# A fused decoder step on one core: first projections from the raw input, norm factor applied to their results, convolution stores moved to GpSimd

## The reference, cut to what matters

```python
xn = rmsnorm(x, g_attn_norm)                     # x * r * g,  r = rsqrt(mean(x*x) + eps), per row
z = jnp.einsum('bsd,de->bse', xn, w_in)          # qa, ka, va, oa, ia, fa, cq, ckv, kr, gate_a, gate_b
q_b = jnp.einsum('bsc,che->bshe', rmsnorm(cq, g_q_a), w_uq)
c_kv = rmsnorm(ckv, g_kv_a); k_rope = rope(kr, pos)
...                                              # mLSTM branch, latent attention branch, gates, W_out
u = jnp.einsum('bsd,df->bsf', rmsnorm(h, g_ffn_norm), w_up)
ext = jnp.concatenate([prev, u], axis=1)         # causal convolution of width 3
out = jnp.einsum('bsf,fd->bsd', silu(gate) * val, w_down)
return x + f, ..., ext[:, -2:]                   # the last two rows are the new convolution state
```

## Time and profile before

| | |
|---|---|
| median of 3 runs | 2778.37 us (2778.24 to 2780.13) |
| profiled execution | 2775.73 us, span 2773.9 us |
| PE busy | 98% (19156 instructions) |
| DVE, ACT, POOL busy | 59%, 46%, 15% |
| mean granted clock of PE | 0.995 |
| first 16 products of the warm-up | 2.88 to 11.68 us |
| DMA | 393.53 MB, mean 142 GB/s |

### The profile page before, as it was taken

How to read it: one execution, slowest core, us unless ns; L and a number is a source line. 1 busy time by engine, 2 the same in 40 slices (tenths; PEclk the granted TensorE clock), 3 DMA queues, 4 the chain that set the end, 5 groups by cost and what they waited for, 6 DMA issues and landing times.

```text
span 2773.9 us, 54080 instructions
## 1 busy us (share of the span) xinstructions
PE 2731.4 (98%) x19156; PEld 2603.6 (94%) x19156; DVE 1640.6 (59%) x2739; ACT 1281.2 (46%) x2286; POOL 404.3 (15%) x762
## 2 busy tenths in 40 slices
PE   9998899999999999999999999999999999999999
PEld 9865799999999979999999999999999999999999
DVE  5466776666666654555454344466677645677744
ACT  5536665565556544444453333344444433444422
POOL 0102343343334310000000000022000000000000
PEclk9999899999999999999999999999999999999999
DMA  7524112212122177656567576576555556555475
GB/s 240 199 70 107 38 46 55 67 49 61 50 63 63 38 236 208 198 171 188 179 177 208 162 172 169 166 192 176 165 165 158 146 164 188 167 162 165 140 175 133
DMA packets 743252, 393.53 MB, mean 142 GB/s; under 512 B 115374, under 2 KB 725400, under 8 KB 742456
## 3 DMA queue, kind: packets, MB, share of 16 engines
q1 hardware_dynamic: 709132, 378.61, 47.6%
q10 hardware_dynamic: 33916, 12.35, 1.7%
HBM read 370.49 MB, written 22.75 MB: 142 GB/s over the span
## 4 chain that ended last, share of the span: by engine, by line
PE 59%; DVE 1%; ACT 1%; issue 1%; ACTq 1%; DMA 0%; SPq 0%; DVEq 0%
PE bank L302 19%; PE bank L307 19%; PE bank L303 19%; DMA stage<-in_w_in_dram 0%; PE bank L2748 0%; ACT sqm L2812 0%; PE bank L2726 0%; PE bank L2736 0%; ACTq L3382 0%; DVE hn L2913 0%; ACT w_hi_b L283 0%; PE bank L2733 0%; ACTq L3383 0%; PE bank L2722 0%; ACTq L3388 0%
## 5 line engine op out<-in xcount | busy, mean ns | idle before, releaser
L290 DVE TENSOR_TENSOR w_lo_b<-stage,w_hi_b 128x2048 fp32r<-128x2048 f32 (+2 forms) x286 | 612.4, 2142 | 411.2 <-ACT w_hi_b L283 407.2
L283 ACT ACTIVATE w_hi_b<-stage 128x2048 fp32r<-128x2048 f32 (+1 forms) x284 | 508.1, 1790 | 568.0 <-PE bank L307 509.0
L302 PE MATMUL bank<-xnH,w_hi_b 128*128 128x288 f32 (+1 forms) x2736 | 741.1, 299 | 2.7 <-PEq L191 2.5
L303 PE MATMUL bank<-xnL,w_hi_b 128*128 128x288 f32 (+1 forms) x2736 | 735.7, 295 | 0.0
L302 PEld LDWEIGHTS bank<-xnH,w_hi_b 128*128 128x128 f32 (+1 forms) x2736 | 514.0, 188 | 12.4 <-issue 11.4
L303 PEld LDWEIGHTS bank<-xnL,w_hi_b 128*128 128x128 f32 (+1 forms) x2736 | 513.4, 188 | 0.3
L1741 PE MATMUL bank<-uk_all,lat 128*128 128x384 f32 (+1 forms) x1344 | 441.4, 328 | 13.2 <-DVE lat L2535 5.3
L1743 PE MATMUL bank<-uk_all,lat 128*128 128x384 f32 (+1 forms) x1344 | 435.1, 324 | 0.0
L307 PE MATMUL bank<-xnH,w_lo_b 128*128 128x288 f32 (+1 forms) x2736 | 390.8, 295 | 0.0
L307 PEld LDWEIGHTS bank<-xnH,w_lo_b 128*128 128x128 f32 (+1 forms) x2736 | 372.1, 188 | 0.0
L302 PE MATMUL bank<-haH,w_hi_b 128*128 128x288 f32 x1024 | 275.3, 296 | 4.7 <-ACT w_hi_b L283 4.7
(11 more groups left out here) (535 smaller groups left out, 3707.7 us busy)
## 6 DMA issues: line engine op xcount, KB each, us to landing
stage<-in_w_in_dram SPq DMA_DIRECT2D x88, 1024.0 KB, 5.3
stage<-in_w_up_dram SPq DMA_DIRECT2D x88, 1024.0 KB, 5.3
stage<-in_w_down_dram SPq DMA_DIRECT2D x64, 704.0 KB, 4.7
raw<-in_cache_kv_latent_dram SPq DMA_DIRECT2D x256, 64.0 KB, 1.8
stage<-in_w_branch_a_dram SPq DMA_DIRECT2D x16, 1024.0 KB, 5.5
stage<-in_w_branch_b_dram SPq DMA_DIRECT2D x16, 1024.0 KB, 5.4
stage<-in_w_out_dram SPq DMA_DIRECT2D x16, 1024.0 KB, 5.7
vals<-in_cache_kv_latent_dram SPq DMA_DIRECT2D x60, 256.0 KB, 2.9
```

Of the source, the lines that this page charges most:

```text
L283: act.activation(h, a, ACT.Copy).then_inc(w_hi, 1)
L290: dve.tensor_tensor(lo, a, h.bitcast(F32), ALU.subtract).then_inc(w_lo, 1)
L302: pe.matmul(out, hi, xH(k), start=first and k == 0, stop=False)
L303: pe.matmul(out, hi, xL(k), start=False, stop=False)
```

## The change

- The warm-up is 6 products, and the two behind the gain rows go. `turn_x` transposes plain x (one instruction for each of three tiles, `is_transpose`), with no factor r. SP's order is: identity, first feature half of x, sample rows, first half of block 0's weights, second feature half of x, second half of block 0's weights, then the two gain rows, then blocks 1 to 3.
- Blocks 0 to 8 are formed from g * x without r. In the loop over chunks block 1 lags by 12; block 2's high products stand behind block 0's low ones.
- The squares, the root, the reciprocal and the diagonals come later (`norms` on ACT behind block 2's split). A product of ones with the diagonals spreads r over all partitions in bank 4, and DVE copies it to `rx`.
- DVE multiplies each result by `rx` as it reads the bank (`scaled_out`), and ACT squares the scaled one in SBUF (`square`).
- The normed x is made afterwards in four groups of four chunks: GpSimd adds high and low part and multiplies by `rx`, ACT rounds to the new high part, DVE subtracts, and SP stores the halves in eight pieces between the query chunks. ACT's first query evacuation waits for these stores, since the high parts lie in x_reg.
- The transposes of the convolution state lie two each behind the first two blocks of the first pair; its eight stores are issued by GpSimd as soon as they are done.

```diff
@@ SP
+                    x_half(0)
                     sp.dma_start(x_tok[0:N_S, 2, :], A["x_sample"]...).then_inc(x_in2, 16)
+                    first_weights(0, w_first)
+                    x_half(1)
+                    first_weights(1, w_landed[0])
                     sp.wait_ge(rows_zero, 1)
...
-                    chunk(0)
-                    chunk(1)
-                    for i in range(2, 6):
+                    def normed(g):
+                        part = slice(g * XG, (g + 1) * XG)
+                        sp.wait_ge(x_nL, g + 1)
+                        sp.dma_start(xnL_dram[:, part, :], xr[:, part, :]).then_inc(xL_out, 16)
+                        sp.wait_ge(x_nH, g + 1)
+                        sp.dma_start(xnH_dram[:, part, :], xrH[:, part, :].bitcast(F32)).then_inc(xH_out, 16)
+                    for i in range(4):
                         chunk(i)
-                    sp.wait_ge(x_L, KC)
-                    sp.dma_start(xnL_dram, xnL[:].bitcast(F32)).then_inc(xL_out, 16)
-                    chunk(6)
-                    sp.wait_ge(x_H, KC)
-                    sp.dma_start(xnH_dram, xnH[:].bitcast(F32)).then_inc(xH_out, 16)
+                        normed(i)
@@ PE
-                    warm(16)
+                    warm(6)
                     pe.wait_ge(rows_in, 16 * 9)
                     pe.transpose(bank[3][:, 0:60], rows[:], ident[0:60, 0:60]).then_inc(vec_t, 1)
-                    warm(2)
...
-                            tr = pe.matmul(bank[4 + c % 4][:, t0:t0 + n], x_tok[:, t, chunk_], norm_t[:, t, 0:n], start=True, stop=True)
+                            if c % (KC // 2) == 0:
+                                pe.wait_ge(x_in[t][c // (KC // 2)] if t < 2 else x_in2, 16)
+                            tr = pe.transpose(bank[4 + c % 4][:, t0:t0 + n], x_tok[0:n, t, chunk_], ident[0:n, 0:n])
...
+                    for k in range(KC):
+                        pe.wait_ge(x_L, k + 1)
+                        if k + 4 < KC:
+                            turn_x(k + 4)
+                        high_half(0, k)
+                        if k >= LAG:
+                            high_half(1, k - LAG)
+                    for k in range(KC - LAG, KC):
+                        mm = high_half(1, k)
+                    mm.then_inc(x_hb, 1)
+                    low_half(0)
+                    for k in range(KC):
+                        high_half(2, k)
+                    low_half(1)
+                    low_half(2)
+                    pe.wait_ge(x_dg, 3)
+                    pe.matmul(bank[4][:, 0:T], ones, rw[:, 0:T], start=True, stop=True).then_inc(x_rb, 1)
...
-                            pe.wait_ge(z_free[c], i + 1)
+                            pe.wait_ge(c_sq, LC * i + c + 1)
@@ ACT
                     for c in range(KC):
                         high(c)
+                        if c in (1, 4, 8, 11):
+                            quarter_high(0, (1, 4, 8, 11).index(c))
+                    for g in range(4):
+                        quarter_high(2, g)
+                    norms()
...
+                    def square(m):
+                        act.wait_ge(z_free[m % 4], m // 4 + 1)
+                        if m >= 4:
+                            act.wait_ge(a_sum, 1)
+                        act.activation(sqc[:, m % 4, :], (cqT if m < 4 else ckvT)[:, m % 4, :], ACT.Square).then_inc(c_sq, 1)
+                    def normed_high(g):
+                        act.wait_ge(x_nr, g + 1)
+                        act.activation(xrH[:, part, :], xr[:, part, :], ACT.Copy).then_inc(x_nH, 1)
                     for n in range(4, 9):
                         split_hi(act, At(n), width=W0 if n == 8 else P)
-                        small(n - 2)
+                        square(n - 2)
+                        if n > 4:
+                            normed_high(n - 5)
...
+                    square(7)
                     uq_high(0)
-                    small(8)
                     uq_high(1)
                     act.wait_ge(x_out, 32)
+                    act.wait_ge(xL_out, 16 * 4)
+                    act.wait_ge(xH_out, 16 * 4)
@@ GpSimd
+                    pool.wait_ge(x_L, KC)
+                    pool.wait_ge(x_ss, 5)
+                    for g in range(4):
+                        part = slice(g * XG, (g + 1) * XG)
+                        pool.tensor_tensor(xr[:, part, :], xnH[:, part, :].bitcast(F32), xnL[:, part, :].bitcast(F32), ALU.add).then_inc(x_sum, 1)
+                        pool.wait_ge(x_rx, 1)
+                        pool.wait_ge(x_sum, g + 1)
+                        pool.tensor_tensor(xr[:, part, :], xr[:, part, :], rx[:].unsqueeze(1).broadcast_to([P, XG, T]), ALU.mult).then_inc(x_nr, 1)
@@ DVE
                     for n in range(3, 9):
                         split_lo(dve, At(n), width=W0 if n == 8 else P)
+                        if n == 3:
+                            dve.wait_ge(x_rb, 1)
+                            dve.tensor_copy(rx[:], bank[4][:, 0:T]).then_inc(x_rx, 1)
+                            dve.wait_ge(x_rx, 1)
+                            scaled_out(0)
+                            scaled_out(1)
+                        else:
+                            scaled_out(n - 2)
+                        if n > 4:
+                            normed_low(n - 5)
                         if n == 6:
                             latent(0, cqT, G_QA)
...
+                    scaled_out(7)
                     uq_low(0)
+                    scaled_out(8)
                     uq_low(1)
@@ last stage: ACT, GpSimd, DVE
-                            if g and c.i is None and c.c == 2:
-                                conv_out(m)
...
+                pool.wait_ge(c_ev, 4)
+                for q in range(4):
+                    pool.dma_start(conv_s[q], rin[32 * q:32 * q + 2 * NB]).then_inc(cvs_out, 16)
+                    pool.dma_start(conv_p[q], rin[32 * q + CR:32 * q + CR + 2]).then_inc(cvs_out, 16)
...
-                            if g and c.i is None and c.c == 0:
+                            if g and c.i is None and c.c == 0 and m < 2:
                                 dve.wait_ge(u_new, 4 * GRP)
-                                part = slice(m * CQ, (m + 1) * CQ)
-                                dve.transpose(rin[:, part]..., cv[:, part]...).then_inc(c_ev, 1)
+                                for i in (2 * m, 2 * m + 1):
+                                    part = slice(i * CQ, (i + 1) * CQ)
+                                    dve.transpose(rin[:, part]..., cv[:, part]...).then_inc(c_ev, 1)
```

133 lines of the change are left out of this document (57 added, 76 removed).

## The result

The changed kernel takes 2789.11 us in the median (2787.21 to 2793.3, 6 runs), the kernel before 2778.3 (2775.76 to 2782.48, 6 runs): a ratio of 1.0039 (95% interval 1.0027 to 1.0051). It is slower by 10.8 us. The forecast of 2779.2 was 10 us too low, and its range ended at 2787.5. The profiled execution took 2788.91 us with a span of 2787.1, that is 13.2 more span than the profile of before.

The account below looks back on a forecast made before the run. PE, busy 98% of the span, was taken to bound the kernel. The terms -3.8 + 2 + 8.4 + 1 - 6.8 = +0.8 us gave 2776.5 profiled, 2779.2 for a median, range 2771.5 to 2787.5.

Parts of the forecast that it names:

- What bounds the kernel: Whole kernel: PE is busy 98% of the span, so the end moves only by what makes PE do less or wait.
- Work taken off PE: Ahead of block 3: plain transposes at 0.11 us each, 0.33 a turn, make twelve turns cost 4.0 us, not 7.9.
- Start: First turns wait for gain rows landing at 13.3 us; first product at 15.4, block 3 at 39.0, 3.8 earlier.
- rival C: SP's gain rows don't wait behind the weights, turns start near 8 us: -6.2 us, 2772.2; chance 0.05.
- The clock at the start: PE idles from 6.2 to 13.3 us after the shorter warm-up, lowering the clock: +2 us, bounds 0 and 3.3.
- Norm factor and halves: Block 3 to queries: GpSimd and DVE take turns, PE waits 8.4 us more (5.5 to 9.8), plus 1 of clock.
- the 1 before block 8: A PE wait of 1 us before block 8, part of the 8.4 us of new waits.
- Rival B: GpSimd and DVE don't hold each other up in the new order: -8.1 us, 2770.3; chance 0.15.
- Convolution stores: Near the end: eight stores leave ACT's queue, whose issuing delayed PE: gain 6.8 us, bounds 0 and 6.8.
- Rival A: GpSimd's stores take no less from the path, PE waits for weights there: +7.6 us, 2786.0; chance 0.17.
- The sum: All terms together: +0.8 us, 2776.5 for a profiled execution and 2779.2 for a median; forecast's chance 0.55.
- What would show it: Signs in the new trace: block 3's start, stretched low halves, two PE waits, low clock, ACT's issue waits, low-half spacing.

Follow-up runs that it names:

- e5_full_turns: The changed kernel with 24 warm-up products and the third transpose of each turn on 128 rows instead of 32: 2776.13 us, one run.
- e7_rows_first: The changed kernel with SP loading its two gain rows right behind the identity, six warm-up products as in the changed kernel: 2782.97 us, one run.
- e1_warm24: The changed kernel with 24 warm-up products of PE instead of six, nothing else: 2780.52 us, ratio 1.0008 to the kernel before.
- e6_before_short_warm: The kernel before with six warm-up products instead of sixteen, nothing else: 2776.35 us, one run.
- e9_cold_full: The changed kernel with its six warm-up products and the third transpose of each turn on 128 rows: 2777.49 us, one run.

## Why the prediction was wrong, point by point

- **What bounds the kernel.** PE, and the end moves with its start and its waits: right.
- **Work taken off PE** (twelve turns from 7.9 to 4.0). Wrong. 0.11 each is right for transposes with 128-row weights (0.33 a turn in e5_full_turns), but the row it was scaled from the earlier trace rows has no change of row count in it. With the 32-row third one a turn costs 0.59, so twelve are 7.1 and the gain 0.8.
- **Start** (rows at 13.3, first product at 15.4). That the rows come late for their place in SP's order was right (e7_rows_first), and rival C was out. They landed 1.5 later than worked out, and not for the reason given, transfers in order: SP's issue of the first took 4.16, and the second landed 5.1 behind its own issue. With the dearer turns the first product came at 17.9 at full clock (e1_warm24), and block 3 at 43.9 instead of 39.0.
- **The clock at the start** (+2, bounds 0 and 3.3). The step that failed: the clock's loss measured 10.1 us (54.0 less the 43.9 of e1_warm24), three times its upper bound. The bound let about as long a stretch of work run at the low level as PE had been idle, as the earlier trace rows had it, where dense products follow the idle time (its 6.6 us are 7.1 by the prediction's own 6.2 and 13.3). The prediction said itself that no row shows how soon the clock returns, and bounded it all the same; no rival stood for a longer stay. Here the clock stayed low for as long as the loop ran, 25 us. The bound should have been the whole loop at the low level. With 128-row weights the term would have been about right: 3.5 in e6_before_short_warm, 1.7 in e9_cold_full.
- **Norm factor and halves** (8.4, bounds 5.5 to 9.8, and +1 of clock): right in mechanism and place; the size is partly luck. GpSimd's instructions took 2.68 (forecast 2.65), DVE's splits 4.37 to 4.66, PE's waits 2.0 and 3.4 (forecast 3.7 and 3.6; the 1 before block 8 didn't come). These are 5.4, just under the lower bound; the rest of the 7.7 is mostly the low clock behind the first wait (about 1.9, an estimate from the 0.48 instead of 0.27 between products up to 74 us). With the 1.3 behind the second the clock took 3.2 where +1 stood, near its bound of 3.4. So waits too dear and clock too cheap gave 9.0 against 9.4. The stores of the halves cost PE nothing (forecast 0, at most +1): ACT's 3.8 before its first evacuation was for PE's late query product. Rival B was out.
- **Convolution stores** (-6.8, bounds 0 and -6.8): right, -7.1 in the trace and -6.8 by themselves. Rival A was out.
- **The sum**: +0.8 forecast, +13.2 measured. Block 3 came at +11.2 instead of -1.8: 10.1 for the clock, and +1.1 for turns and rows where -3.8 stood. All later terms together, +2.6 forecast, gave +2.0. The 2.6 us added to go from a profiled execution to a median turned out at 0.2 (2788.91 to 2789.11), which hid 2.4 us of the miss.
- **What would show it.** "A granted clock below 1 in 13 to 20 us" was asked for; it was below 1 to 40. The stretched low halves, the two waits of PE and the 4.39 between its low halves at the end came as written. Two signs did not: block 3 near 39 to 41 (54.0), and no issue wait of ACT above 1 us after 2640. There were three, up to 5.4 and 14.6 in all, and PE didn't wait for them.

## What to carry to other kernels

Before taking fill-in work of PE away, bound what the clock costs by the whole stretch until dense products begin, not by the length of the idle time, and keep the weights of a dense loop at one number of rows, padded with zeros if need be. Count work given to GpSimd as time taken from DVE: here DVE did the same eight instructions itself in half the time and the chain was 7 us shorter, while cutting them in pieces only changed who waits. And a wait of PE costs its length and the clock behind it: 5.4 us of waits cost 3.2 more.

## What the runs showed of the hardware that I had not expected

- One weight load of 32 rows among loads of 128 costs 0.26 us a step at full clock, and after idle time the granted clock stayed at 0.50 for 25 us with it (21 with products in place of transposes, though the 32-row weights went on behind that); full rows, with more columns to move, let it return within 6 us of the first turn.
- GpSimd's copies from one source hold off DVE, and are held off by it, as its two-source instructions do (1.15 became 3.21); and DVE's instruction of one column took 2.62 behind GpSimd.
- The same addition of 1152 columns takes 2.68 on GpSimd and 1.35 on DVE.
